# Which rows of an expert's block the consecutive tokens take: a new table of constants

## What is computed

```python
def _moe(h, grp_w, grp_b, exp_w, exp_b, w_gate, w_up, w_down):
    # h: (n_tok, 1024); 4 groups of 8 experts; each token takes 2 experts of its best group
    ...
    wts = (g_w[:, None] * e_p / jnp.sum(e_p, axis=-1, keepdims=True)).reshape(-1)
    eid = (g_sel[:, None] * EXPERTS_PER_GROUP + e_i).reshape(-1).astype(jnp.int32)
    ...
    def run(args):                      # one block of one expert
        tok, wt, e = args
        xb = h_pad[tok]                 # gather rows of 1024 floats
        hid = jax.nn.silu(xb @ w_gate[e]) * (xb @ w_up[e])     # 1024 -> 512
        return (hid @ w_down[e]) * wt[:, None]                 # 512 -> 1024
    ...
    out = jnp.zeros((n_tok + 1, d), h.dtype).at[buf_tok].add(ys.reshape(cap, d))
```

```
layer 0: 14 30 16 26 13 30 42 31 32 49 20 26 20 54 46 67 16 46 16 18 31 44 23 48 44 18 62 35 34 19 21 33
layer 1: 17  7 13 18 24 19 31 13  5 10 10 11 12 10 16  4 27 23 18 18 21 25 10  8 13 10 25 28 17 18 21 10
```

## Time and profile before

| | |
|---|---|
| time, 3 runs | 2209.35 us median (2206.35 to 2213.73) |
| profiled execution, span | 2211.1 us |
| PE busy (matmul) | 2040.4 us (92%) |
| PEld / DVE / ACT / POOL busy | 1068.5 / 960.5 / 423.0 / 239.1 us |
| moved by DMA | 635.70 MB, mean 288 GB/s |
| mixture of layer 0, about | 1043 to 1560 us |
| mixture of layer 1, about | 1718 to 2200 us |

### The profile page before, as it was taken

The page is one execution under the profiler, slowest core; times in us unless marked ns, Lnnn a source line. Parts: engine busy times, 40 slices in busy tenths (PEclk is TensorE's granted clock), DMA queues, the critical chain, the costliest instruction groups (busy, mean ns, idle before and its releaser), DMA issues.

```text
span 2211.1 us, 22906 instructions
## 1 busy us (share of the span) xinstructions
PE 2040.4 (92%) x8736; PEld 1068.5 (48%) x8736; DVE 960.5 (43%) x1864; ACT 423.0 (19%) x917; POOL 239.1 (11%) x305
## 2 busy tenths in 40 slices
PE   9989999999899998999988989888888998999997
PEld 5456666445666576445433433333454433433332
DVE  5757996763999618944211101210643210111212
ACT  3241000233100214743000000000342100000001
POOL 1010000000000104310211111110000111111110
PEclk9999999999999999999999989999999899999989
DMA  8663888454588603024999999999926799999996
GB/s 298 220 241 111 323 327 291 172 187 156 203 309 314 237 20 124 29 86 145 381 397 417 394 408 407 397 404 399 355 82 225 303 419 421 373 411 420 405 416 270
DMA packets 132089, 635.70 MB, mean 288 GB/s; under 512 B 15908, under 2 KB 18260, under 8 KB 104480
## 3 DMA queue, kind: packets, MB, share of 16 engines
q1 hardware_dynamic: 109072, 575.10, 66.5%
q0 software_dynamic: 19360, 37.21, 5.0%
q10 hardware_dynamic: 3568, 22.21, 2.7%
HBM read 630.70 MB, written 29.52 MB: 299 GB/s over the span
## 4 chain that ended last, share of the span: by engine, by line
PE 70%; DMA 19%; DVE 7%; ACT 2%; issue 2%; SPq 0%; POOL 0%; DVEq 0%; ACTq 0%
DMA ring<-ex_up 17%; PE PS L1720 16%; PE PS L1290 9%; PE PS L1282 8%; PE PS L697 8%; PE PS L1175 6%; PE PS L1738 5%; PE PS L600 3%; PE PS L1708 2%; PE PS L2874 2%; PE PS L1729 1%; PE PS L1033 1%; PE PS L2905 1%; PE PS L1049 1%; DVE arena L3273 1%
## 5 line engine op out<-in xcount | busy, mean ns | idle before, releaser
L1720 PE MATMUL PS<-ring,arena 128*64 128x512 f32 x960 | 463.1, 639 | 80.3 <-DMA ring<-ex_up 75.9
L1723 PE MATMUL PS<-ring,arena 128*64 128x512 f32 x976 | 470.6, 639 | 0.0
L2179 DVE COPY arena<-PS 128x512 f32<-128x512 f32 x64 | 44.2, 691 | 598.4 <-PE PS L1708 598.4
L1720 PEld LDWEIGHTS PS<-ring,arena 128*64 128x64 f32 x960 | 135.7, 147 | 343.4 <-issue 323.6
L1738 PE MATMUL PS<-ring,arena 128*64 128x512 f32 x992 | 228.2, 602 | 1.6 <-DVE arena L2175 1.6
L1282 PE MATMUL PS<-arena,ring 128*128 128x256 f32 x896 | 198.0, 379 | 0.0
L1282 PEld LDWEIGHTS PS<-arena,ring 128*128 128x128 f32 x896 | 170.2, 190 | 34.2 <-issue 12.4
L1929 ACT ACTIVATE arena<-PS 64x512 f32<-64x512 f32 x65 | 38.2, 588 | 610.7 <-PE PS L1720 583.2
L2279 POOL DMA_INDIRECT arena<-tokens_d,arena x65 | 62.1, 956 | 719.6 <-PE PS L1708 558.3
L1723 PEld LDWEIGHTS PS<-ring,arena 128*64 128x64 f32 x976 | 137.8, 147 | 1.9
L1175 PE MATMUL PS<-ring,arena 128*128 128x512 f32 x288 | 128.6, 599 | 2.5 <-issue 1.7
(11 more groups left out here) (367 smaller groups left out, 2582.0 us busy)
## 6 DMA issues: line engine op xcount, KB each, us to landing
ring<-ex_down SPq DMA_DIRECT2D x62, 2048.0 KB, 22.7
ring<-ex_up SPq DMA_DIRECT2D x59, 2048.0 KB, 22.0
ring<-ex_gate SPq DMA_DIRECT2D x58, 2048.0 KB, 17.6
ring<-ffn_w SPq DMA_DIRECT2D x32, 2048.0 KB, 14.1
ring<-mod_w SPq DMA_DIRECT2D x24, 2048.0 KB, 8.7
ring<-a_w_qkv SPq DMA_DIRECT2D x8, 2048.0 KB, 16.3
ring<-b_w_qkv SPq DMA_DIRECT2D x6, 2048.0 KB, 8.4
ring<-w_in_ab SPq DMA_DIRECT2D x3, 2048.0 KB, 12.1
```

Source lines behind the costliest of these rows:

```text
L1720: g = pe.matmul(PS[0:CAP, u, :], xT[:, k, :], gate[k], start=(k == 0), stop=(k == KD - 1))
L1723: h = pe.matmul(PS[CAP:P, u, :], xT[:, k, :], up[k], start=(k == 0), stop=(k == KD - 1))
```

## The change

The table `slot` is no longer 0 to 63. A new function makes a permutation, and column c now takes the rank that the table gives for it.

```diff
+def rank_of_column():
+
+    queues = list(range(0, 16, 2)) + list(range(1, 16, 2))
+    columns = [start + 2 * g for start in (0, 32, 1, 33) for g in queues]
+    return np.argsort(columns)
...
-    parts["slot"] = np.tile(np.arange(CAP), (P, 1))
+    parts["slot"] = np.tile(rank_of_column(), (P, 1))
```

## The result

The changed kernel takes 2195.57 us (median of 6 runs, 2193.77 to 2196.69). Its ratio to the kernel before is 0.9935, with a 95% interval of 0.9921 to 0.9949: some 14 us saved, faster by more than the 0.3% that can be told. The ratio is not the quotient of the two medians that stand beside each other in this run: there the kernel before had 2205.91 us (2204.93 to 2213.73), which is 10.3 us more and a quotient of 0.9953. In the three later sets of runs it had 2209.56, 2209.95 and 2209.65, so I take 2209.6 as its time and the ratios for the savings: 0.0065 x 2209.6 = 14.4 us. Of all runs in this document one, of experiment 5, was slow (2520.21 us at a lower clock), and its ratio leaves it out. The prediction was 2201 us, a saving of 8.4 us, with a range from 2194 to 2211.

A forecast was written before the change was run, and what follows sets the result against it. Weight tiles landing with the slowest DMA engine were taken as the bound. Savings of 4.7 us in layer 0 and 4.1 in layer 1, together 8.8, took the 2211.1 us span to 2202.3, median 2201; range 2194 to 2211.

The forecast's parts named there:

- What bounds the kernel: In most of both mixtures, how soon a 2 MB weight tile lands, with the slowest of 16 DMA engines.
- The map of columns on engines: In gathers engine g has columns 2g, 2g+1, 32+2g, 33+2g, neighbouring pairs together; in scatters four neighbouring partitions share an engine.
- F: Both mixtures: a column's engine is its number modulo 16, giving 12 us and 8.7 us, 2230 us; chance 0.02.
- What a row costs its engine: Both mixtures: each 4 KB gathered row or scattered packet costs its own engine 0.16 us, range 0.15 to 0.21.
- How much reaches the end: Layer 0's whole 4.7 us counts; in layer 1 about 0.68 of 6.1 us, 4.1 us; together 8.8 us.
- The rates and waits: Layer 0's rate rises from 405 to 409 GB/s; PE's `ex_up` waits shrink some 5 us there, 3 to 4 in layer 1.
- A: Both mixtures: evening out small transfers spares the fullest engine, 8.8 us saved, 2201 us; chance 0.60.
- E: In gathers the memory port limits, so rows count by groups of four columns; 15.1 us saved, 2194 us; chance 0.08.
- B: Weight stream: engines wait for a common limit, not their own work, so nothing changes, 2209 us; chance 0.14.
- D: Gathers of experts under 32 tokens bunch, disturbing all engines; doubled, 15.8 us against 8.8 gained, 2216 us; chance 0.07.
- C: Both mixtures: PE's clock falls and takes what DMA gives, half the gain stays, 2205 us; chance 0.09.
- The memory port: In gathers, four neighbouring columns may share a port on which engine 0 also delivers weights; 2194 us, chance 0.08.

The follow-up runs named there:

- experiment 5: Table against the kernel before: consecutive rank pairs keep neighbouring columns, so only the scatter and column groups get half the change; 2201.74 us, ratio 0.996.
- experiments 4 to 12: Nine kernels with other rank tables, four of them with scatters moving nothing, each against the kernel before; 2183.58 to 2246.39 us.
- experiments 9, 11 and 12: Scatters moving nothing, against the kernel before: old table 2196.57 us, packed table 2216.98 us, engine 0 packed with old column groups 2203.94 us.
- experiments 2 and 3: New table in one layer only, against the kernel before: layer 0 alone 2201.33 us, 0.9968; layer 1 alone 2201.60 us, 0.9965.
- experiment 12: Scatters moving nothing, engine 0 packed with ranks 0 to 3 but the old table's column groups kept, against the kernel before; 2203.94 us, ratio 0.9975.
- experiment 4: Packed table against the kernel before: ranks 0 to 3 on engine 0, 4 to 7 on engine 1, and so on; 2246.39 us, ratio 1.0169.
- experiment 7: Changed kernel with odd engines taking their second column pair first, same counts per engine, against the kernel before; 2196.58 us, ratio 0.9942.
- experiment 8: Changed kernel with odd experts dealt from the table's other end, five short VectorE operations a layer added, against the kernel before; 2195.02 us, ratio 0.9929.

## Why the prediction was right or wrong

**What bounds the kernel** was right. The time followed how the rows fall on the engines, in both directions, with the same instructions: 14 us faster with the new table, 37 us slower with the packed one. The drain became steeper as forecast, 2.35 and 1.7 us of mean idle time in two profiles where 1.5 to 2 was said.

**The map of columns on engines** held for the gather: a gather of 7 rows starts on four, seven and two engines under the three tables. All counts of experiments 4 to 12 are made with it, and the signs and most of the sizes come out: +32 us worked out for the packed table, +37.3 measured. For the scatter the four partitions an engine were taken from the rule and only the time bears them out. F, another map, would have made the changed kernel slower by its own sum.

**What a row costs its engine** is the step that failed. The term "each gathered row 0.16 us, on its own engine" was complete for what engine 0 brings itself (0.08 + 0.08 us by experiments 9, 11 and 12) and counted nothing for its neighbour's rows, which land in the columns of engine 0's weights and cost it 0.08 us each. The fullest engine was spared not only its 13 and 16 rows but also 21 and 31 rows of its neighbour. The terms of 4.7 us in layer 0 and 4.1 us in layer 1 came out as 7.1 and 7.7 (experiments 2 and 3), or as 8 and 7 by the intervals. The largest part of what was missing is these neighbours' rows: 21 x 0.08 + 31 x 0.08 x 0.7 = 3.4 us. The rest, 2 to 3 us, stays open.

**How much reaches the end** was not tested by itself. Layer 1's 8.6 us by the prices above came out as 7.7, a share of 0.9 rather than 0.68, which intervals of 3 us don't tell from 0.7; and the prices were found with 0.7 put in. Nothing else became late in place of the gain: TensorE's waits for `ex_up` fell by 11.1 us over the run (7.9 in the second profile), and 15.9 us lie between the gathers.

**The rates and waits** were of the right kind. In layer 0 the rate went from 405 to 408 GB/s (409 in the second profile) where 409 was said, and the waits fell by 4.5 and 5.8 us in the two profiles where 5 was said. In layer 1 they fell by 6.7 and 4.0 us, and 3 to 4 was said. So these signs came as forecast though the saving was larger; they don't show the missing part, and the chain's share, which was to shrink, was 50.5% and 59.0% against 52.0%. As many small packets, more of them of 2 KB, was right: 132089 packets and 104480 under 8 KB in both, with 14852 under 512 B where the page of before has 15908. The 1056 fewer tiny packets fit the prediction: two joined half rows, so far one packet of 4 KB and a tiny one, are two of 2 KB now.

**The rivals.** A had the right mechanism and 60% of the size. E had the right total (2194 against 2195.6) for a reason that is half right: it charged the group only, and experiment 12 shows 7 us where it says nothing. Its sum also took the scatter's counts for the gather and so left out the last two experts; with the gather's own groups (34 and 47 rows less) it is 15.6 us and not 15.1. I gave E 0.08 because a gather slows all engines, which says nothing about a further cost on a single one. B fell with experiment 4, and F with the result. D fell with the result and experiment 7. C, that TensorE takes half of what DMA gives, didn't come: more than the forecast gain stayed, and TensorE's clock rose from 0.94 to 0.96 in the first stretch of layer 1. But experiment 8 is of this kind or of B's: past the changed table the engines are even enough that something else sets the time.

**The memory port.** That the cost on the neighbour is one of a shared port into the on-chip memory was argued and not shown. The Trainium skill, page "SBUF — State Buffer", section "Door 1: The DMA port swizzle", states that partitions 4k to 4k + 3 and 32 + 4k to 32 + 4k + 3 share one port, and these are the groups counted here. The runs agree with these groups: 82 and 124 more rows in engine 0's group cost 13 us with its own rows unchanged. They can't tell the port from anything else that the two engines share by columns, nor from a cost between engines of neighbouring numbers: under the map engines 0 and 1 are both, and no table here takes them apart.

## What to carry to other kernels

When a stream of weights is bound by DMA, count the small transfers on the engine that has most of them, and not their sum: a table of constants that spreads them cost no instruction and gave 0.65%, and packed them the wrong way it cost 1.7%. Count indirect rows on the engine that brings them and on the engine that loads the same columns. Here, once the drain at the stream's end was down to some 2 us, more evenness gave nothing more. And take a second profile of the same kernel before you read a difference: here a chain's share moved from 50.5% to 59.0% with nothing changed.

## What the runs showed of the hardware

- Beside a full stream of weights a gathered 4 KB row cost engine 0 0.08 us when engine 0 brought it (7 us for 83 rows), and 0.08 us when it landed in the columns of engine 0's weights (13 us for 169 rows). These are averages over two layers; by layer they lie between 0.03 and 0.15, and between 0.07 and 0.12 us.
- A gather into 64 partitions spreads its rows by pairs of neighbouring columns: 7 rows in neighbouring columns start as 4 and 3, in columns 4 apart all 7 within 0.15 us, and in columns 0, 1, 32, 33, 2, 3, 34 as 2 and 5.
- The spread of such rows moved the whole stream of weights: 389 GB/s packed, 405 as before, 408 spread out, from 1110 to 1520 us in layer 0, with a DMA share between 0.98 and 1.01. The share of busy time doesn't show that an engine is held up.
- What the scatters cost depends on how they fall on the engines. Their bytes are 5.92 MB (635.70 less 629.78 on the pages), and if all 16 engines shared them evenly that would be 5.92 MB x 37.6 us per MB / 16 = 13.9 us. Left out, they gave back 13 us with the old table, 10 to 12 with the new one (2193.10 and 2195.57 less 2183.58), and 29.4 with the packed one (2246.39 less 2216.98). Counted on engine 0 at 0.16 us it would be 20, 15 and 32 us. So engine 0's count has the order right and is too large by 3 to 7 us.
